# An opening in pairs of modulation chunks: shifts weighed as rows on TensorE, and the second projection chunk split ahead of keys, angles and gates

## What is computed

```python
c_act = silu(c)
mod = c_act @ w_ada[l] + b_ada[l]          # 1024 -> 6 * 1024
sh1, sc1, gt1, sh2, sc2, gt2 = split(mod, 6)
h = rms_norm(x, norm_mix[l]) * (1.0 + sc1) + sh1
proj = h @ w_in[l]                         # queries, keys, values, gates, keys and values of a second attention
```

## Time and profile before

| | |
|---|---|
| median of three runs | 2267.3 us (2265.6 to 2268.5) |
| profiled execution | 2264.2 us, its span 2262.4 us |
| TensorE busy | 2165.1 us, 96% |
| VectorE, ScalarE, GpSimd busy | 1506.6, 1073.5, 563.0 us |
| read from HBM | 380 MB, 169 GB/s over the span |
| s1's matmuls | 46.0 to 55.1 us |

### The profile page before, as it was taken

One profiled execution on the slowest core, in us unless ns is written; L12 is line 12 of the kernel. 1 busy time (PEld: TensorE's weight loads), 2 busy tenths in 40 slices (PEclk: granted clock), 3 DMA queues, 4 the chain that ended last, 5 costly groups with the idle time before them and its releaser, 6 DMA issues.

```text
span 2262.4 us, 39808 instructions
## 1 busy us (share of the span) xinstructions
PE 2165.1 (96%) x17241; PEld 2075.5 (92%) x17241; DVE 1506.6 (67%) x1866; ACT 1073.5 (47%) x1414; POOL 563.0 (25%) x274
## 2 busy tenths in 40 slices
PE   7999999999999999999999999989999999989999
PEld 7988889899988888989999999879999999869999
DVE  6877676787677776667666556776556556686554
ACT  2666563433456647444345335454445344545333
POOL 0873314899248250375000000000000000000000
PEclk7999999999999999999999999999999999989999
DMA  9752335677566224566555555325555555425553
GB/s 292 243 172 88 113 112 188 226 253 241 192 188 205 93 68 145 165 218 204 172 186 172 184 186 170 109 76 185 186 187 169 186 187 168 131 75 161 180 184 128
DMA packets 332856, 383.93 MB, mean 170 GB/s; under 512 B 12551, under 2 KB 315402, under 8 KB 332554
## 3 DMA queue, kind: packets, MB, share of 16 engines
q1 hardware_dynamic: 332234, 381.23, 52.4%
q10 hardware_dynamic: 448, 0.16, 0.0%
HBM read 380.32 MB, written 1.05 MB: 169 GB/s over the span
## 4 chain that ended last, share of the span: by engine, by line
PE 76%; DVE 11%; ACT 8%; issue 3%; SPq 1%; DMA 0%; ACTq 0%; DVEq 0%
PE bank L734 16%; PE bank L736 16%; PE bank L735 16%; DVE weights_low L1363 5%; PE bank L963 5%; PE bank L964 5%; PE bank L965 5%; ACT weights_high L2071 4%; DVE arena L1465 1%; PE bank L748 1%; SPq L666 1%; PE bank L1000 1%; PE bank L1160 1%; PE bank L1145 1%; PE bank L763 1%
## 5 line engine op out<-in xcount | busy, mean ns | idle before, releaser
L1363 DVE TENSOR_TENSOR weights_low<-ring,weights_high 128x2048 fp32r<-128x2048 f32 x302 | 752.1, 2490 | 444.9 <-ACT weights_high L2071 444.5
L734 PE MATMUL bank<-h_high,weights_high 128*128 128x256 f32 x3296 | 943.9, 286 | 23.7 <-DVE weights_low L1363 14.6
L735 PE MATMUL bank<-h_low,weights_high 128*128 128x256 f32 x3296 | 927.0, 281 | 0.0
L736 PE MATMUL bank<-h_high,weights_low 128*128 128x256 f32 x3296 | 926.6, 281 | 0.0
L2071 ACT ACTIVATE weights_high<-ring 128x2048 fp32r<-128x2048 f32 x302 | 578.1, 1914 | 708.1 <-PE bank L736 546.7
L734 PEld LDWEIGHTS bank<-h_high,weights_high 128*128 128x128 f32 x3296 | 621.6, 189 | 41.9 <-DVE weights_low L1363 22.0
L735 PEld LDWEIGHTS bank<-h_low,weights_high 128*128 128x128 f32 x3296 | 622.5, 189 | 3.9 <-issue 3.8
L736 PEld LDWEIGHTS bank<-h_high,weights_low 128*128 128x128 f32 x3296 | 622.4, 189 | 0.0
L963 PE MATMUL bank<-hidden_high,weights_high 128*128 128x256 f32 x1056 | 299.1, 283 | 1.3 <-DVE hidden_low L1605 0.8
L964 PE MATMUL bank<-hidden_low,weights_high 128*128 128x256 f32 x1056 | 298.4, 283 | 0.0
L965 PE MATMUL bank<-hidden_high,weights_low 128*128 128x256 f32 x1056 | 298.4, 283 | 0.0
(11 more groups left out here) (422 smaller groups left out, 2838.3 us busy)
## 6 DMA issues: line engine op xcount, KB each, us to landing
ring<-in_w_in SPq DMA_DIRECT2D x80, 1024.0 KB, 5.3
ring<-in_w_up SPq DMA_DIRECT2D x44, 1024.0 KB, 5.2
ring<-in_ffn_w_gate SPq DMA_DIRECT2D x44, 1024.0 KB, 5.4
ring<-in_ffn_w_up SPq DMA_DIRECT2D x44, 1024.0 KB, 5.3
ring<-in_ffn_w_down SPq DMA_DIRECT2D x44, 1024.0 KB, 5.0
side<-in_w_ada SPq DMA_DIRECT2D x42, 1024.0 KB, 7.7
ring<-in_w_down SPq DMA_DIRECT2D x22, 1024.0 KB, 5.0
ring<-in_w_dn_out SPq DMA_DIRECT2D x8, 1024.0 KB, 5.2
```

The source lines that it names most:

```text
L734: mm(o[:, m, :], a_, high[:, t, :], start=(t == 0), stop=False)
L735: mm(o[:, m, :], a_, low[:, t, :], start=False, stop=False)
L736: last = mm(o[:, m, :], b_, high[:, t, :], start=False, stop=(t == KT - 1))
L1363: v.tensor_tensor(low, wide(q), high.bitcast(F32), ALU.subtract).then_inc(chunk_split, 1)
```

## The change

Chunks of the modulation are loaded and used in pairs, shift i with scale i, for i = 0 to 3. The order of loads is shift 0, scale 0, s1 (the three ring slots), then shift and scale 1 and 2 (`start_at`), qkv0, and shift and scale 3 (the side buffers), with small loads between. TensorE weighs a shift as a row (`weigh_row`): a column of `ccol` is stationary and 256 columns of the chunk move, eight matmuls; ScalarE copies the row out (`row_out`), and TensorE turns it to two columns (`columns`). VectorE weighs all scales (`modulate`). `modulate_pair` makes two tiles' shift and scale at a time, `head_rounded` and `low_tiles` the high and low halves of h, and `head_tiles` the matmuls of s1 for two tiles, both halves of the tokens. The product with rinv is one operation for all tiles. qkv0 is split on both engines before the last pair of tiles. In both layers qkv1 is now split before keys and gates are staged; in layer 0 the angles follow the gate sums. The third side load waits for the last row, the fourth for the last scale. The core of the diff:

```diff
...
-ADA_V = (4, 6, 7, 0)
-ADA_RING = (5, 1)
+ADA_V = (1, 5, 2, 6)
+ADA_RING = (0, 4)
+EARLY = 9
...
-SIDE = [(0, 2), (0, 3)] + [(0, i) for i in range(8, 24)] + [(1, i) for i in range(24)]
+SIDE = [(0, 3), (0, 7)] + [(0, i) for i in range(8, 24)] + [(1, i) for i in range(24)]
...
             def load_side(j):
                 l, i = SIDE[j]
-                if j >= 2:
-                    sp.wait_ge(side_summed, j - 1)
+                if j == 2:
+                    sp.wait_ge(row_weighed, 4)
+                elif j == 3:
+                    sp.wait_ge(chunk_modulated, 4)
+                elif j >= 4:
+                    sp.wait_ge(side_summed, j - 3)
...
+            load_chunk(0)
+            load_chunk(1)
+            load_chunk(2)
+            load_rows(ACT_LOADS, ACT_LOADS + 5)
             load_start(0)
-            load_chunk(0)
-            load_rows(ACT_LOADS, ACT_LOADS + 5)
+            load_rows(ACT_LOADS + 5, ACT_LOADS + 10)
             load_start(1)
-            load_rows(ACT_LOADS + 5, ACT_LOADS + 10)
-            load_side(0)
             load_rows(ACT_LOADS + 10, ACT_LOADS + 15)
             load_start(2)
             load_rows(ACT_LOADS + 15, ACT_LOADS + 20)
+            load_start(3)
+            load_rows(ACT_LOADS + 20, N_IN)
+            load_chunk(NS)
+            load_side(0)
             load_side(1)
-            load_rows(ACT_LOADS + 20, N_IN)
-            load_start(3)
-            load_chunk(1)
-            load_chunk(2)
+            sp.dma_start(K[:, 2 * P:C_COL], a["shape_constants"][:, 2 * P:C_COL]).then_inc(k_landed, 16)
             for q in range(NS, len(chunks)):
-                load_chunk(q)
-                if q == NS:
-                    sp.dma_start(K[:, 2 * P:C_COL], a["shape_constants"][:, 2 * P:C_COL]).then_inc(k_landed, 16)
+                if q > NS:
+                    load_chunk(q)
                 for j in side_at.get(q, ()):
...
-                pe.wait_ge(side_summed, 4 * n - 2)
+                pe.wait_ge(side_summed, 4 * n - 4)
...
+            def weigh_row(i):
+                if i == 0:
+                    q = Q["ada", 0, ADA_RING[0]]
+                    pe.wait_ge(w_landed[q % NS], landed[q])
+                    w = slot(q)[:, 0:2 * D].rearrange("p (t n) -> p t n", t=KT)
+                elif i < 3:
+                    pe.wait_ge(start_landed[2 * i - 2], 16)
+                    w = start_at[2 * i - 2]
+                else:
+                    pe.wait_ge(side_landed[0], 16)
+                    w = side[0][:, :].rearrange("p (t n) -> p t n", t=KT)
+                if i >= 2:
+                    pe.wait_ge(row_copied, i - 1)
+                row = B[3][0:1, (i % 2) * T:(i % 2) * T + T]
+                for t in range(KT):
+                    last = mm(row, ccol[:, t:t + 1], w[:, t, :], start=(t == 0), stop=(t == KT - 1))
+                last.then_inc(row_weighed, 1)
+            def columns(i):
+                shift, scale = (L[R["adr", 0, g] % 2] for g in range(2))
+                pe.wait_ge(row_copied, i + 1)
                 for m in range(2):
-                    at = 2 * (c % 4) + m
-                    for t in range(KT):
-                        last = mm(L[r % 2][:, STEP * at:STEP * at + 1], w[:, t, m * P:(m + 1) * P], ccol[:, t:t + 1], start=(t == 0), stop=(t == KT - 1))
-                last.then_inc(used, 1)
-            def weigh_ring(c):
-                q = Q["ada", 0, c]
-                pe.wait_ge(w_landed[q % NS], landed[q])
-                weigh_start(c, slot(q)[:, 0:2 * D].rearrange("p (t n) -> p t n", t=KT), chunk_weighed)
-            def reduce_start(g, made):
-                r = R["adr", 0, g]
-                for c in made:
-                    for m in range(2):
-                        at = 2 * (c % 4) + m
-                        last = mm(L[r % 2][:, STEP * at:STEP * at + 1], acc[:, g, at * P:(at + 1) * P], ones[:, 0:1], start=True, stop=True)
-                last.then_inc(mod_summed, 1)
+                    at = STEP * (2 * i + m)
+                    last = mm(shift[:, at:at + 1], modrow[0:1, i % 2, m * P:(m + 1) * P], ones[0:1, 0:1], start=True, stop=True)
+                last.then_inc(shift_summed, 1)
+                pe.wait_ge(chunk_modulated, i + 1)
+                for m in range(2):
+                    at = STEP * (2 * i + m)
+                    last = mm(scale[:, at:at + 1], acc[:, 1, (2 * i + m) * P:(2 * i + m + 1) * P], ones[:, 0:1], start=True, stop=True)
+                last.then_inc(scale_summed, 1)
+            def head_tiles(*tiles):
+                n = SI["s1", 0, 0]
+                wh, wl = halves(n)
+                pe.wait_ge(chunk_split, n + 1)
+                for t in tiles:
+                    pe.wait_ge(norm_ready, t + 1)
+                    for tt in range(2):
+                        a_, b_ = h_high[:, t, tt * P:(tt + 1) * P], h_low[:, t, tt * P:(tt + 1) * P]
+                        to = B[4 + tt][:, 0:WIDE]
+                        mm(to, a_, wh[:, t, :], start=(t == 0), stop=False)
+                        mm(to, a_, wl[:, t, :], start=False, stop=False)
+                        last = mm(to, b_, wh[:, t, :], start=False, stop=(t == KT - 1))
+                if tiles[-1] == KT - 1:
+                    last.then_inc(chunk_multiplied, 1)
...
-            weigh_ring(5)
             pe.wait_ge(x_done, 4)
+            weigh_row(0)
             for u in range(4):
                 sum_pair(0, u)
-            for j in range(2):
-                pe.wait_ge(side_landed[j], 16)
-                weigh_start(SIDE[j][1], side[j][:, :].rearrange("p (t n) -> p t n", t=KT), side_summed)
-            pe.wait_ge(inputs_landed, 16 * N_IN)
-            for v in range(8):
+            pe.wait_ge(vectors_landed, 16 * (EARLY - 1))
+            tr(B[0][:, 0:V_ROWS[0]], rowst[0:V_ROWS[0], 0, :], ident[0:V_ROWS[0], 0:V_ROWS[0]]).then_inc(vectors_turned, 1)
+            columns(0)
+            weigh_row(1)
+            columns(1)
+            head_tiles(0, 1)
+            weigh_row(2)
+            columns(2)
+            head_tiles(2, 3)
+            pe.wait_ge(inputs_landed, 16 * (N_IN - EARLY + 1))
+            for v in range(1, 8):
                 n = V_ROWS[v % 3] if v < 6 else V_ROWS[3]
                 tr(B[v // 4][:, (v % 4) * P:(v % 4) * P + n], rowst[0:n, v, :], ident[0:n, 0:n])
             mm(B[2][:, P:P + R_ALL], ones[0:1, :], hrow[0:1, 0:R_ALL], start=True, stop=True)
             pe.wait_ge(start_v, 1)
             mm(B[2][:, T:2 * T], ones[0:1, :], posf[0:1, :], start=True, stop=True).then_inc(start_transposed, 1)
-            pe.wait_ge(chunk_modulated, 5)
-            reduce_start(0, (0, 1))
-            reduce_start(1, (4, 6, 7))
+            weigh_row(3)
+            columns(3)
+            head_tiles(4, 5)
+            head_tiles(6, 7)
             for l in range(LAYERS):
-                special("s1", l, 2 * l)
+                if l:
+                    special("s1", l, 2 * l)
                 for i in range(12):
...
+            def modulate_pair(i):
+                shift, scale = (L[R["adr", 0, g] % 2][:, STEP * 2 * i:STEP * (2 * i + 2):STEP] for g in range(2))
+                two = lambda at: slice(at + 2 * i, at + 2 * i + 2)
+                dve.wait_ge(shift_summed, i + 1)
+                ins = v.tensor_tensor(modc[:, two(0)], shift, vcol[:, 0, two(0)], ALU.add)
+                if i < 3:
+                    then(ins)
+                else:
+                    ins.then_inc(mod_ready, 1)
+                dve.wait_ge(scale_summed, i + 1)
+                ins = v.tensor_tensor(modc[:, two(KT)], scale, vcol[:, 0, two(KT)], ALU.add)
+                if i < 3:
+                    then(ins)
+                else:
+                    ins.then_inc(mod_ready, 1)
+                    dve.wait_ge(mod_ready, 2)
+                v.scalar_tensor_tensor(out=scol[:, two(0)], in0=modc[:, two(KT)], scalar=1.0, in1=vcol[:, 0, two(VA["norm_mix"])],
+                                       op0=ALU.add, op1=ALU.mult).then_inc(pair_modulated, 1)
+            def low_tiles(i):
+                for t in (2 * i, 2 * i + 1):
+                    dve.wait_ge(h_rounded, t + 1)
+                    v.tensor_tensor(h_low[:, t, :], tmp[:, t, :], h_high[:, t, :].bitcast(F32), ALU.subtract).then_inc(norm_ready, 1)
...
             modulate(0)
+            dve.wait_ge(vectors_turned, 1)
+            then(v.tensor_copy(vcol[:, 0, 0:V_ROWS[0]], B[0][:, 0:V_ROWS[0]]))
+            dve.wait_ge(norm_factor, 1)
+            v.tensor_tensor(tmp[:, :, :], x[:, :, :], over(rinv[:, :], KT), ALU.mult).then_inc(x_normed, 1)
+            modulate_pair(0)
             modulate(1)
+            split(1)
+            low_tiles(0)
+            modulate_pair(1)
             modulate(2)
-            dve.wait_ge(inputs_landed, 16 * N_IN)
+            low_tiles(1)
+            dve.wait_ge(inputs_landed, 16 * (N_IN - EARLY + 1))
             v.tensor_copy(posf[0:1, :], posi[:, :]).then_inc(start_v, 1)
+            modulate_pair(2)
```

(69 more changed lines are left out.)

38 lines of the change are left out of this document (19 added, 19 removed).

## The result

The changed kernel takes 2272.45 us (median of 13 runs, 2270.2 to 2274.5), the kernel before 2265.55 us (13 runs beside them). The ratio is 1.0029, with a 95% interval of 1.0021 to 1.0036: **slower by 0.3%**. The forecast was 2264.4, a gain of 2.9 us against a median of 2267.3; the change cost 6.9 us. The profiled executions say the same: span 2262.4 us before, 2269.8 us after, 7.4 us more.

A forecast was written before the change was run, and what follows sets the result against it. TensorE, busy nearly throughout, bounds the kernel, so the gain is qkv2's earlier start: 2.5 us, plus 0.4 in layer 1, 2.9 off 2267.3 gives 2264.4 us. Range 2261.3 to 2274.5, the forecast's own 2262.8 to 2266.3.

The forecast's parts named there:

- the last row's end: Opening, TensorE: row 3 of the shifts ends at 46.5 us, releasing SyncE's third side load and the qkv1 and qkv2 loads.
- GpSimd's start: Opening: GpSimd starts at 59.6 us, after the gate sums, 2.2 us later than before, and delays nobody.
- the rows lift the clock: Opening, TensorE: 256 moving columns raise the clock despite one stationary column; a row then takes 3.5 us, not 6.9.
- Rival 2: Opening rows do not hold the clock, row 3 ends at 57.5 at most; 7 us late, 2274.3 us, chance 0.22.
- The dry stream: Sign in the opening: loads wait for row 3, so DMA share is near zero for two us before 46 to 47.
- The step that failed: Layer 0, VectorE: the angles, 2 us, cost nothing while it waits for ScalarE, unless qkv2's split comes sooner.
- charged the meeting to the split: Layer 0, VectorE: qkv2's split takes 3.9 us, not 2.3 alone, because GpSimd is at work.
- a break of TensorE between 70 and 120 us: Sign that the forecast is wrong: TensorE stops in this stretch, where it had no break before.
- 0 to 1 us of slack: VectorE's splits after qkv2 have this slack against TensorE; a first stall of up to 1 us is in range.
- 0.4 us for layer 1: Layer 1: the earlier split of qkv1 removes TensorE's 0.44 us wait, winning no more than 0.4 us.
- the forecast 2.5 us for qkv2: Layer 0, TensorE: qkv2 can start at 66.8 us instead of 69.3, a gain of 2.5 us.
- The rival of a fuller gain: Opening: clock up from 34 us, qkv2's split meets no GpSimd operation; gain 5.2 to 5.6, 2261.5 us, chance 0.20.

The follow-up runs named there:

- Experiment 8: experiment 1 with the shifts weighed in the old form, 32 matmuls of one moving column, without row copies and turning: 2271.87 us, ratio 1.0032 to the kernel before.
- experiment 1: The changed kernel with layer 0's angle operations, except the change of sign, moved ahead of VectorE's split of qkv1: 2263.2 us, ratio 0.9989 to the kernel before.
- Experiment 2: The changed kernel with GpSimd's first operation also waiting for the last angle operation, VectorE's order unchanged: 2263.42 us, ratio 0.9987 to the kernel before.
- experiment 7: experiment 1 with SyncE's third side load issued behind the loads of qkv1 and qkv2: 2263.45 us, ratio 0.999 to the kernel before.
- experiment 6: The changed kernel with 44 unread matmuls on TensorE ahead of qkv2 in layer 0: 2268.75 us, ratio 1.0017 to the kernel before.
- experiment 4: The changed kernel without its second part, so qkv1 is again split behind angles and gates: 2268.37 us, ratio 1.0013 to the kernel before.
- experiment 5: experiment 4 with GpSimd's first operation waiting for VectorE's split of qkv1: 2265.51 us, ratio 0.9997 to the kernel before.

## Why the prediction was wrong, and where it was right

**The opening of the profiled execution came as forecast to half a microsecond, down to the split of qkv1.** The change was forecast to put the last row's end at 46.5 (46.3), SyncE's third side load at 46 to 47 (46.38), the landing of qkv1 at 54.8 (54.85), its low half at 59.1 (59.1), GpSimd's start at 59.6 (59.67) and the rounding of qkv2 at 62.9 (62.5). The rows took 3.61 us at the full level (forecast 3.5) and 3.98 for row 2 (4.5). The choice behind it, that the rows lift the clock, fits this execution: clock 1.00 through rows 0, 1 and 3, and in row 2 it rose. Rival 2 fell: its price, 2274.3, is near the measured time, but its mechanism did not happen, as row 3 ended at 46.3 and not at 57.5. Experiment 8 shows what hung on the choice, 8.7 us. That the half microsecond was met is in part luck: row 2, which was put at 4.5 us "as the clock rises in it", took 3.71 to 5.07 us in the seven kernels that have these rows, and row 0 took 5.4 to 5.7 us in three of them (experiments 1, 2 and 7). The prediction also weighed the Trainium skill, "TensorE: Matmul & The Clock Gate", section "HAM oscillation — how this bites in real kernels", by which all rows would have been at the low level. The groups of that section stand between waits longer than the groups themselves. The opening did not have that shape: groups of 2.8 to 8.4 us stood between waits of 0.4 to 1 us and kept 1.00, and only the stretch from about 28.2 to 35 us was low, behind a wait of 2.5 us. The dry stream was seen too: DMA share 0.04 at 41.5 to 45 us.

**The step that failed** is a term that the sum put at nothing, in the sentence "The angles (2 us) lie on VectorE while it waits for ScalarE: free, unless the split of qkv2 comes sooner." The window was long enough, 59.4 to 62.5; the work in it was not 2 us but 9.0 us (59.37 to 68.35). The prediction knew that GpSimd starts just before and charged the meeting to the split (3.9 us for 2.3), but not to the six small operations in front of it. They depend on each other, GpSimd has operations of 0.8 to 2.4 us back to back, and from the second on each small one was held by one of them. In numbers: the split started 5.5 us later than forecast (68.38 for 62.9) and took 1.6 less (2.29 for 3.9, GpSimd being done by then), so qkv2 started 3.9 us late, at 70.73 for 66.8. Experiment 2 takes the meeting away and experiment 1 moves the work in front of it: qkv2 then starts at 66.84 and at 66.53, and the totals are 9.0 and 9.2 us lower.

**What was missed behind it.** The prediction named a break of TensorE between 70 and 120 us as a sign of being wrong, and it came. First, an idle time of 5.64 us lets the clock fall: 2.4 us over the next chunk, 2.0 of them back in experiment 6. Second, VectorE had 0 to 1 us of slack in the prediction; the waits between 75 and 115 us cost 1.7. Third, the sum handed on a gain or a loss in the opening one to one, with 0.4 us for layer 1 (measured 0.6, and the wait of the earlier trace rows is gone). The +1.6 us near 215 us, and the 4.3 us early that experiment 7 lost again to 0.7, show that this isn't so.

**The counterfactual gain.** With the failed step repaired, the forecast 2.5 us for qkv2 was met (69.3 to 66.53 or 66.84), and the total against before was 2.5 and 2.9 us less by the ratios (0.9989 and 0.9987, each with some 2 us of interval to either side): the sum of 2.9 us is then in keeping with the runs. The way there was not the forecast's, though: the trace of experiment 1 is 2.7 us ahead at 75 us, 1.8 at 126, 2.4 behind the start of layer 1, 1.5 us late at 1500 and 0.8 ahead at the end, so that the total agrees is in part luck. The rival of a fuller gain (qkv2 at 64.1) did not come true even in experiment 7, where TensorE's own work sets 65.1, and the total stayed at 2263.45.

**What stays open** is why the clock falls or not at the distant places, and how much of the loss belongs to them in the median of many runs; the steps were read from one profiled execution of each kernel.

## What to carry to other kernels

When small, dependent VectorE operations are moved behind the point that starts GpSimd, price each of them at the length of the GpSimd operation that it meets, not at its own, and look in the trace at both engines' lists side by side. An idle time of TensorE of some microseconds can be paid twice, once as it passes and once in the slow matmuls behind it (5.64 us and then 2.4 us here). Before a gain in the opening is handed on to the end of a long kernel, check where else TensorE stands still briefly: those places may give it back.

## What the runs showed of the hardware

- In the kernel after, rows of one stationary column and 256 moving ones ran at a granted clock of 1.00 (16 records in 3.61 us), and the clock rose from 0.50 within row 2. In experiment 8, with 32 matmuls of a full stationary tile and one moving column in their place, the clock was 0.50 from 42 to 55 us (6.82 to 6.99 us a shift) although the engine shows no gap.
- The granted clock of the profile and the pace of the matmuls do not always agree early in a trace. Row 0 of experiment 1 has no gap and a granted clock of 1.00, and yet its first seven records last 624 ns on average, for 378 in the kernel after. In these rows of groups (count, busy time and mean duration), the first is experiment 1 in 12.2 to 15 us, the second the kernel after in 12.1 to 15.7:

```profile
L1032 PE MATMUL bank<-ring,ccol 128*1 128x256 f32 x7 | 3.1, 624 | 0.8 <-DVE x L1710 0.8
...
L1032 PE MATMUL bank<-ring,ccol 128*1 128x256 f32 x16 | 3.6, 378 | 0.8 <-issue 0.8
```

- A TENSOR_SCALAR of 128x256 with one input in SBUF was held as long (2.35 us for 0.29) as operations with two such inputs (2.00 to 2.16 us for 0.43).
- The moment at which the clock rises within one row is not the same from run to run: row 2 took 3.71 to 5.07 us in seven kernels with the same list up to it (3.71, 3.98, 4.52 and 5.07 in experiment 4, the kernel after, experiments 7 and 5), and row 3 behind it started between 42.40 and 44.20 us.
